# A fourth of the eight late modulation panels multiplied by VectorE instead of TensorE, and the sum of the last one moved behind four convolution chunks

## The reference: what is computed

```
mod = SiLU(cond) @ w_mod + b_mod   -> shift1, scale1, gate1, shift2, scale2, gate2
h   = RMSNorm(x) * (1 + scale1) + shift1
z   = h @ w_in                     -> q, k, v, B, C, u
o   = concat(differential_attention(q, k, v), B * conv3(C * u)) @ w_o
x   = x + gate1 * RMSNorm(o)
h   = RMSNorm(x) * (1 + scale2) + shift2
x   = x + gate2 * RMSNorm(HierMoE(h))
```

## Time and profile before

| | |
|---|---|
| median of three runs | 722.8 us (720.81 to 724.8) |
| the profiled execution | 720.89 us |
| its span, first to last instruction | 719.0 us |
| mean granted TensorE clock | 0.987 of full speed |
| TensorE busy | 674.5 us (94%) |
| VectorE busy | 523.0 us (73%) |
| ScalarE busy | 418.7 us (58%) |
| GpSimd busy | 76.4 us (11%) |

### The profile page before, as it was taken

One profiled execution on the slowest core, in us unless ns is written; L12 is line 12 of the kernel. 1 busy time (PEld: TensorE's weight loads), 2 busy tenths in 40 slices (PEclk: granted clock), 3 DMA queues, 4 the chain that ended last, 5 costly groups with the idle time before them and its releaser, 6 DMA issues.

```text
span 719.0 us, 11065 instructions
## 1 busy us (share of the span) xinstructions
PE 674.5 (94%) x3604; PEld 540.2 (75%) x3604; DVE 523.0 (73%) x749; ACT 418.7 (58%) x626; POOL 76.4 (11%) x132
## 2 busy tenths in 40 slices
PE   3899999989999999989999999999999999999984
PEld 0567766669999986767889788888888888877841
DVE  2546785766455566664478898889999998988938
ACT  5542222233534646875362568888888888888733
POOL 2020001154000000000000200000000111120050
PEclk9899999999999999999999999999999999999998
DMA  9944787759322230300629699999999999999783
GB/s 340 387 168 148 280 263 246 243 174 330 89 75 65 86 141 12 116 1 14 250 109 331 251 355 398 398 399 398 399 398 398 398 399 398 398 398 398 319 291 147
DMA packets 89640, 187.07 MB, mean 260 GB/s; under 512 B 7251, under 2 KB 20616, under 8 KB 89604
## 3 DMA queue, kind: packets, MB, share of 16 engines
q1 hardware_dynamic: 78896, 154.69, 59.1%
q0 software_dynamic: 6688, 20.89, 8.1%
q10 hardware_dynamic: 4022, 11.05, 3.9%
HBM read 166.64 MB, written 19.96 MB: 260 GB/s over the span
## 4 chain that ended last, share of the span: by engine, by line
PE 65%; DMA 13%; DVE 10%; ACT 5%; issue 3%; SPq 3%; POOL 1%; POOLq 0%; ACTq 0%; DVEq 0%
PE ps L1771 15%; DMA raw_ring<-in_w_exp_down 10%; PE ps L1568 8%; PE ps L1603 7%; PE ps L1791 7%; PE ps L1619 6%; PE ps L1604 5%; PE ps L1501 3%; PE ps L1660 2%; PE ps L1635 2%; DMA raw_ring<-in_w_in 2%; DVE split_ring L1216 1%; PE ps L1456 1%; PE ps L1651 1%; PE ps L1753 1%
## 5 line engine op out<-in xcount | busy, mean ns | idle before, releaser
L1771 PE MATMUL ps<-split_ring,split_rows 128*128 128x512 f32 x768 | 179.1, 392 | 2.5 <-DVE steer L1353 0.9
L1771 PEld LDWEIGHTS ps<-split_ring,split_rows 128*128 128x128 f32 x768 | 142.7, 188 | 33.5 <-DVE split_ring L1216 2.4
L1216 DVE TENSOR_TENSOR split_ring<-qkv_mem,split_ring 128x1024 fp32r<-128x1024 f32 x128 | 148.4, 1218 | 16.1 <-ACT split_ring L776 15.9
L776 ACT CAST split_ring<-qkv_mem 128x1024 fp32r<-128x1024 f32 x128 | 127.5, 1055 | 17.6 <-ACT catT_mem L859 9.2
L1603 PE MATMUL ps<-split_rows,split_ring 128*128 128x384 f32 x288 | 87.7, 345 | 0.8 <-DVE catT_mem L1122 0.4
L1791 PE MATMUL ps<-split_ring,split_rows 128*128 128x512 f32 x360 | 85.6, 393 | 0.0
L1216 DVE TENSOR_TENSOR split_ring<-raw_ring,split_ring 128x1024 fp32r<-128x1024 f32 x64 | 75.8, 1220 | 7.0 <-ACT split_ring L776 5.9
L1604 PE MATMUL ps<-split_rows,split_ring 128*128 128x256 f32 x288 | 80.5, 279 | 0.0
L1791 PEld LDWEIGHTS ps<-split_ring,split_rows 128*128 128x128 f32 x360 | 66.5, 188 | 13.1
L607 ACT CAST split_ring<-raw_ring 128x1024 fp32r<-128x1024 f32 (+1 forms) x36 | 33.5, 953 | 71.8 <-DMA raw_ring<-in_w_in 60.0
L776 ACT CAST split_ring<-raw_ring 128x1024 fp32r<-128x1024 f32 x64 | 64.5, 1050 | 10.3 <-DMA raw_ring<-in_w_exp_down 10.3
(11 more groups left out here) (312 smaller groups left out, 894.9 us busy)
## 6 DMA issues: line engine op xcount, KB each, us to landing
qkv_mem<-in_w_exp_gate SPq DMA_DIRECT2D x64, 512.0 KB, 12.5
qkv_mem<-in_w_exp_up SPq DMA_DIRECT2D x60, 512.0 KB
raw_ring<-in_w_exp_down SPq DMA_DIRECT2D x60, 512.0 KB, 13.1
raw_ring<-in_w_mod SPq DMA_DIRECT2D x32, 512.0 KB, 4.9
qkv_mem<-in_w_mod SPq DMA_DIRECT2D x16, 512.0 KB, 11.4
expert_rows<-catT_mem ACTq DMA_DIRECT2D x15, 512.0 KB, 6.7
raw_ring<-in_w_in SPq DMA_DIRECT2D x12, 512.0 KB, 6.6
raw_ring<-in_w_in SPq DMA_DIRECT2D x48, 128.0 KB, 2.7
```

The costliest lines, as they stand in the source:

```text
L776: nc.scalar.copy(spl[:, moe_split_slot(tile, j, r), 0, :], moe_raw(tile, j, r)).then_inc(S["hi"], 1)
L1216: tt(spl[:, slot, 1, :], moe_raw(tile, j, r), spl[:, slot, 0, :].bitcast(F32), ALU.subtract).then_inc(S["lo"], 1)
L1771: ins = mm(ps[:, j, :], xS[:, s, k, :], spl[:, slot, m, (k % 2) * N:(k % 2 + 1) * N], start=(k == 0 and s + m == 0), stop=(k == KC - 1 and ...
```

## The change

`BY_ROWS` becomes (5, 7, 9, 11), so panels 5, 7, 9 and 11 are multiplied by VectorE, and 4, 6, 8 and 10 by TensorE. There are eight halves instead of ten, and 16 quarters for VectorE instead of 12. The tables of halves, rows and sums are rewritten, and with them the order of the ring. The sums of a VectorE panel lie in other banks and rows. The sum of panel 11 leaves the end of the loop and goes behind four chunks of the first convolution group; `scores(0)` comes three chunks later, and one chunk is left behind it.

```
-        BY_ROWS = (6, 9, 11)
+        BY_ROWS = (5, 7, 9, 11)
...
-        HALVES = {3: 0, 4: 1, 5: 2, 6: 3, 7: 6, 8: 7, 9: 8, 10: 9, 11: 12, 12: 13}
-        ROWS = {4: ((6, 0),), 5: ((6, 1),), 6: ((6, 2),), 7: ((6, 3),), 8: ((9, 0),), 9: ((9, 1),), 10: ((9, 2),),
-                11: ((9, 3), (11, 0)), 12: ((11, 1),), 13: ((11, 2), (11, 3))}
-        SUM_AT = {5: 4, 7: 5, 8: 6, 9: 7, 11: 8, 12: 9, 13: 10, 14: 11}
+        HALVES = {3: 0, 4: 1, 6: 4, 7: 5, 8: 8, 9: 9, 10: 12, 11: 13}
+        ROWS = {3: ((5, 0),), 4: ((5, 1),), 5: ((5, 2), (5, 3)), 6: ((7, 0),), 7: ((7, 1),), 8: ((7, 2), (7, 3)), 9: ((9, 0),),
+                10: ((9, 1),), 11: ((9, 2), (9, 3)), 12: ((11, 0), (11, 1)), 13: ((11, 2), (11, 3))}
+        SUM_AT = {5: 4, 6: 5, 8: 6, 9: 7, 10: 8, 12: 9, 13: 10, 14: 11}
...
-            return {6: 6, 9: 7, 11: 3}[c] if c in BY_ROWS else 2 + BY_MM.index(c) % 2
+            return {5: 6, 7: 7, 9: 6, 11: 2}[c] if c in BY_ROWS else 2 + BY_MM.index(c) % 2
...
-                    if n < 2:
-                        pe.wait_ge(S["roped"], 3)
-                    else:
-                        pe.wait_ge(S["mod_row"], BY_MM[3] - MOD_EARLY + 1)
+                    pe.wait_ge(S["roped"], 3)
+                    if n >= 2:
+                        pe.wait_ge(S["mod_row"], (5, 8)[n - 2] - MOD_EARLY + 1)
...
-                if g in SUM_AT:
+                if g in SUM_AT and g < 3 * TB - 1:
                     mod_sums(SUM_AT[g])
...
                 if k == 0 and g == 0:
-                    pe.wait_ge(S["roped"], 3)
+                    pe.wait_ge(S["mod_row"], 9 - MOD_EARLY + 1)
...
+            conv_next(4)
+            mod_sums(N_MOD - 1)
             conv_next(3)
             scores(0)
-            conv_next(5)
+            conv_next(1)
```

More of the change, by code:

```diff
@@ L217, in mod_bank @@
         def mod_bank(c):
-            return {6: 6, 9: 7, 11: 3}[c] if c in BY_ROWS else 2 + BY_MM.index(c) % 2
+            return {5: 6, 7: 7, 9: 6, 11: 2}[c] if c in BY_ROWS else 2 + BY_MM.index(c) % 2
         def sums_of_rows(c):
-            o = 1024 * BY_ROWS.index(c)
+            o = (0, 1024, 2048, 4096)[BY_ROWS.index(c)]
             return [catT_mem[:, o + 512 * z:o + 512 * (z + 1)] for z in range(2)]
@@ L1446, in mod_half @@
                         pe.wait_ge(S["hf_ctx"], KC)
-                    elif c == MOD_EARLY + 1:
+                    elif BY_MM.index(c) == 1:
                         pe.wait_ge(S["roped"], 1)
```

## The result

| | before | after |
|---|---|---|
| median | 722.86 us (719.7 to 726.14, 9 runs) | 728.23 us (725.59 to 731.17, 9 runs) |
| ratio, with its 95% interval | | 1.0075 [1.0051, 1.0099] |
| the profiled execution | 720.89 us | 726.22 us |
| its span | 719.0 us | 724.5 us |
| mean granted clock | 0.987 | 0.989 |

What follows compares the result with a forecast made beforehand. TensorE was taken to set the pace, except for one 2.82 us wait for VectorE. Terms summed to +5.05, taken as +4.9 us on a 722.8 median: 727.7 us, with an 8-in-10 range of 723.3 to 731.3.

Steps and rivals of the forecast that it cites:

- TensorE's work: In the loop, two halves go and one sum takes two matmuls for one: -1.1 us.
- the old wait: At the end of the loop, TensorE's idle time ahead of the sum of panel 11 goes: -2.8 us.
- first new wait, step 4: TensorE waits for rotations held behind panel 5's first quarter, whose load lands late: +3.0 us.
- second, sum of panel 7: In step 9, TensorE reaches this sum before VectorE has finished the panel: +1.2 us.
- third, sum of panel 9: In step 12, TensorE waits because VectorE must first split a late-loaded convolution quarter: +2.05 us.
- end of the loop, v copy: After step 14, TensorE waits for ScalarE's copy of the last v block, formerly hidden: +0.7 us.
- behind the scores: Between `scores(0)` and `scores(1)`, one chunk is left to cover the exponentials, leaving part bare: +2.0 us.
- third rival: New TensorE gaps lower its clock once or twice: +6.5 to +8.2 us, 729.3 to 731.0; chance 0.15 shared with late VectorE.
- The mark that I had named for a wrong prediction: A difference at `scores(1)` that isn't there at the end would show the prediction wrong; no size given.
- VectorE keeps up: In the loop, none of the three new waits comes: 721.6 us, or 718.9 if chunk count doesn't matter; chance 0.08.
- Only the first wait: Only step 4's wait comes, as convolution quarters land faster and VectorE catches up: +1.8 us, 724.6; chance 0.15.
- The fourth: TensorE waits for panel 11 at the sum's new place too: 729 us and above; chance 0.15 shared with a clock fall.

Runs made afterwards that it cites:

- third execution of after: The changed kernel profiled a third time with nothing edited; this execution took 726.65 us.
- half-work kernel: The changed kernel with VectorE doing two of the four instructions of every quarter, loads and TensorE's work kept: 723.52 us, ratio 1.0017.
- e1: The changed kernel with panel 5's first quarter moved from step 3 to step 4, behind the two rotations: 728.41 us, ratio 1.008.
- e6: The changed kernel with panel 5's first quarter one step later and 3 chunks, sum of panel 11, 2 chunks, `scores(0)`, 3 chunks: 727.03 us, ratio 1.0061.
- second execution of after: The changed kernel profiled once more with nothing edited; this execution took 732.06 us.
- first, second and sixth experiment: First: e1. Second: the changed kernel with the sum of panel 11 back at the end of the loop, 729.97 us, ratio 1.0088. Sixth: e6.

## Why the prediction was right

In the order of its steps, against the third execution of after and the first of before, neither with a clock fall in the loop:

| step | forecast | measured |
|---|---|---|
| TensorE's work | -1.1 | -0.8 |
| the old wait | -2.8 | -2.8 |
| first new wait, step 4 | +3.0 | +3.15 |
| second, sum of panel 7 | +1.2 | +1.8 |
| third, sum of panel 9 | +2.05 | +1.7 |
| end of the loop, v copy | +0.7 | +0.7 |
| behind the scores | +2.0 | +2.05 |
| `scores(1)` behind `z_rows(3)` | +4.9 | 108.93 - 103.20 = +5.7 |

The first is `z_rows(5)` to `z_rows(14)`, 72.02 against 69.27 us, less the waits in it of 1.80 and 1.72. For the seventh, `scores(0)` to `scores(1)` takes 4.12 us, 1.69 of it idle, where before, less four chunks of 0.95, it took 5.87 - 3.8 = 2.07. The measured rows sum to 5.8. Behind `scores(1)` the difference passes on, as assumed: the rest to the experts is 232.34 against 232.28.

The forecast of 727.7 us against a measured 728.23 is closer than its terms. Three of them were too low, by 0.3, 0.15 and 0.6, and the third wait was too high by 0.35; that they partly cancel is luck.

**TensorE's work** was mis-sized by 0.3. A sum in a step without a half takes 0.95 us (after, L1475 at 147.81 to 148.76), where I had 0.82 from steps with one, and steps with a wait are a little longer beside it: step 9 less its wait takes 10.59 - 1.80 = 8.79 us, where I had 8.72.

**The first new wait** is right in place, cause and size. The load landed at 67.1 where I had 66.84. The half-work kernel still waits 5.03 us for this load and is late in step 4; the early quarter on the kernel before shows the term alone and in full. But it is not a term of its own in the four-panel kernel, as my sum had it. Taken away, it came back at the next sums for the most part (e1) or wholly (e6), since VectorE has next to no slack from there to the sum of panel 7.

**The second** is the term that I mis-sized most: 1.2 against 2.26 in the first execution and 1.80 in the third. The step that failed is "two waits of 0.63 for ScalarE's split as before". VectorE waited 1.11 + 0.73 for splits and 0.28 + 0.45 for loads, 2.57 us, where I had 1.26 (third execution: 1.01 + 0.77 + 0.29 = 2.07). Its own work, which I had at 40.95 us, is borne out: 113.11 - 69.72 - 2.57 = 40.8. As its waits (2.57) are longer than TensorE's (2.26), this wait takes both: work that leaves no slack, and waits on top of it.

**The third**, which I called the least certain, came by the chain that I described. The second convolution quarter's load took 132.28 - 126.46 = 5.8 us from issue to ScalarE's split (I took 5.9), VectorE waited 3.49 for it, and TensorE 1.74.

**The end.** The v copy's 0.7 was 0.67, and the sum of panel 11 found its rows long ready: VectorE ended them at 149.14 + 6.25 = 155.4, and the sum starts at 158.90. The two moved pieces together were to give -2.8 + 0.7 + 2.0 = -0.1 and gave 18.90 - 19.07 = -0.17.

**The clock.** "The granted clock is 1.00 in the loop" was wrong for the profiled execution. My third rival happened beside the forecast: 1.7 us at the sum of panel 7, in two of three executions of this kernel, and 7.86 us in all at `scores(1)`. It did not bring the total to the rival's 729.3 to 731.0. In that execution the 18 matmuls near 279 us ran at full clock, 4.37 us against 5.69 before, which gave 1.3 back (I had read the price of that fall as 1.6). From the experts to the end it took 1.2 less, which I can't put down to the change, as that column differs by 1.5 between repeats of the kernel before. So that this pair of executions differs by 5.5 us is partly chance, while the 5.7 without clock falls and the 5.4 of the medians agree.

The mark that I had named for a wrong prediction, a difference at `scores(1)` that isn't there at the end, did show: 8.0 us there, 5.5 at the end. It did not mean a wrong mechanism. It meant that one execution's clock had been read as the kernel's.

**The other rivals.** "VectorE keeps up" is out: the earlier trace rows had spoken against it, and after it 41.86 of 46 us are busy. By the Trainium skill (Perfetto Trace Analysis, Identifying the Most-Contended Engine) the engine with the highest occupancy is to be optimized first, and TensorE is judged there by the busy time of its weight loads or by its share of the peak, not by the busy time of its matmuls. In this case's trace the weight loads take 75% of the whole span and VectorE 73%, which names TensorE by little; from 67 to 113 us before they take 30.64 of 46 us and VectorE 36.25, which names VectorE, while TensorE's matmuls have no gap. Relieving TensorE of 0.8 us at VectorE's expense gave a ratio of 1.0075, so the occupancy of the whole span was no help here. "Only the first wait" fell with the waits at panels 7 and 9. The fourth, a wait for panel 11 at its new place, is out by 3.5 us.

## What to carry to other kernels

Before work is handed to an engine that looks idle, add up its work between two points at which others wait for it, and its waits; occupancy over the whole span doesn't tell that. VectorE was idle for 27% of the span, and yet had no slack where it counted. Where an engine works in order, an instruction whose data come late belongs behind those that others wait for: one early quarter alone cost 3.16 us. A wait that is taken away ahead of such an engine can come back at the next point where others wait for it. A sum that is moved to hide its wait pays only if the filling work is shared out anew: 3, 2, 3 chunks brought 0.9962 [0.9936, 0.9988], 4, 3, 1 brought 0.9991 [0.9966, 1.0016].

## What the runs showed of the hardware

Behind gaps of 0.9 to 2.8 us TensorE's clock fell in some executions of a kernel and stayed up in others. Behind the gap of 2.22 or 2.23 us near 275 us, in all 14 profiled executions, the 18 matmuls took 4.37 us once and 5.69 to 7.27 in the other thirteen; before, with 5.69, the stretch shows a granted clock of 0.60. The gap at the sum of panel 11 with three panels left the clock at 1.00 once (2.82 us) and lowered it twice (2.55, 2.59). The one at the sum of panel 7 lowered it in the first and second execution of after and in the first, second and sixth experiment (1.93 to 2.67 us), and not in the third execution (1.80). The two gaps of step 4 (the second 1.56 us) lowered it in two of the executions, and the one at the sum of panel 9, 1.64 to 2.35 us, in none. The one of 0.9 us ahead of the experts lowered it in five of fourteen. So the length of the gap alone does not decide, and what else does stays open. A fall costs 1.2 to 2.9 us where it can be read off, about as much as a gap. Whether small matmuls in a gap prevent it stays open: the clock stood in both executions that had them, and in one of the six with four panels, full row work and no fill.

The Trainium skill (TensorE: Matmul & The Clock Gate, What's actually happening) has it that activity lifts a clock that is slow by default; the granted clock of these stretches agrees in that it fell only behind gaps, and in after it was back at 1.00 from 118 us on, once TensorE was busy again.

Between these points the program repeats to less than a tenth of a per cent: from `scores(1)` to the experts, without the 18 matmuls, it took 232.26 to 232.42 us in twelve of the fourteen. The other two, at 233.89, have a slow clock behind the wait for `scores(1)`.
